# Expert blocks ahead of the routing: rounded products whose remainder is made by an accumulating transfer

## The reference, cut to what matters

```python
q = (hf @ wq).reshape(T, PEER_HEADS, 2, PEER_DQ // 2)
s = jnp.einsum('thcd,hckd->thck', q, subkeys)
v_top, i_top = lax.top_k(s, PEER_TOPK)
cand_s = v_top[:, :, 0, :, None] + v_top[:, :, 1, None, :]
best_s, best_pos = lax.top_k(cand_s, PEER_TOPK)
g = jax.nn.softmax(best_s, axis=-1)
ub = jnp.take(u_tab, ids, axis=0)
act = jax.nn.gelu(jnp.einsum('tkd,td->tk', ub, x))
y = jnp.einsum('tk,tkd->td', g * act, jnp.take(v_tab, ids, axis=0))
```

## Time and profile before

| | |
|---|---|
| median of three runs | 2167.39 us |
| the profiled execution | 2171.05 us |
| its span, first to last instruction | 2169.3 us |
| TensorE busy | 2108.0 us, 97% of the span |
| VectorE busy | 1376.8 us, 63% |
| ScalarE busy | 704.3 us, 32% |
| GpSimd busy | 4.8 us |
| mean granted TensorE clock | 0.986 of full speed |

### The profile page before, as it was taken

The page is one execution under the profiler, slowest core; times in us unless marked ns, Lnnn a source line. Parts: engine busy times, 40 slices in busy tenths (PEclk is TensorE's granted clock), DMA queues, the critical chain, the costliest instruction groups (busy, mean ns, idle before and its releaser), DMA issues.

```text
span 2169.3 us, 31600 instructions
## 1 busy us (share of the span) xinstructions
PE 2108.0 (97%) x12416; PEld 1897.5 (87%) x12416; DVE 1376.8 (63%) x1874; ACT 704.3 (32%) x745; POOL 4.8 (0%) x11
## 2 busy tenths in 40 slices
PE   7999998998999998999999999999999999999997
PEld 5888887887988998999999999989999999999785
DVE  6675575568788986556565655655555565654675
ACT  2014112005311344434334343433434334342432
POOL 0000000000000000000000000000000000000000
PEclk8999999999999999999999999999999999999999
DMA  9999595994443458555555555655555565555552
GB/s 390 421 419 362 197 365 236 380 421 172 171 155 116 180 216 319 206 179 209 188 218 193 195 207 176 219 189 207 204 183 207 186 222 189 200 206 177 196 193 78
DMA packets 98649, 496.12 MB, mean 229 GB/s; under 512 B 8256, under 2 KB 41312, under 8 KB 43040
## 3 DMA queue, kind: packets, MB, share of 16 engines
q1 hardware_dynamic: 83280, 373.81, 45.9%
q10 hardware_dynamic: 14112, 115.35, 14.0%
q0 software_dynamic: 1200, 6.16, 0.7%
HBM read 473.14 MB, written 22.15 MB: 228 GB/s over the span
## 4 chain that ended last, share of the span: by engine, by line
PE 89%; DMA 7%; DVE 3%; ACT 1%; issue 0%; ACTq 0%; DVEq 0%; SPq 0%; POOL 0%
PE ps L470 19%; PE ps L459 11%; PE ps L460 11%; PE ps L461 11%; PE ps L725 5%; PE ps L727 5%; PE ps L726 5%; PE ps L714 5%; PE ps L715 5%; PE ps L716 5%; DMA mod_first<-wmod 4%; PE ps L671 3%; DMA mod_ring<-wmod 1%; DVE mod_first L1112 1%; DMA wraw<-wst 1%; DVE rstd L1088 0%
## 5 line engine op out<-in xcount | busy, mean ns | idle before, releaser
L461 PE MATMUL ps<-h_hi,wlo 128*128 128x256 f32 x1952 | 553.3, 283 | 0.0
L459 PE MATMUL ps<-h_hi,whi 128*128 128x256 f32 x1728 | 490.0, 284 | 5.4 <-ACT act_u L954 5.4
L460 PE MATMUL ps<-h_lo,whi 128*128 128x256 f32 x1728 | 490.0, 284 | 0.0
L1411 DVE TENSOR_TENSOR yacc<-yacc,ps 128x512 f32<-128x512 f32 x256 | 176.1, 688 | 404.5 <-PE ps L727 404.5
L461 PEld LDWEIGHTS ps<-h_hi,wlo 128*128 128x128 f32 x1952 | 375.5, 192 | 0.0
L1377 DVE TENSOR_TENSOR vlo<-vraw,vhi 128x2048 fp32r<-128x2048 f32 x116 | 260.8, 2289 | 135.3 <-ACT vhi L1001 135.3
L459 PEld LDWEIGHTS ps<-h_hi,whi 128*128 128x128 f32 x1728 | 332.7, 193 | 7.6 <-issue 5.6
L460 PEld LDWEIGHTS ps<-h_lo,whi 128*128 128x128 f32 x1728 | 332.7, 193 | 2.0
L470 PE MATMUL ps<-hid,wraw 128*128 128x256 f32 x1344 | 296.6, 381 | 4.7 <-DVE hid L1258 4.7
L470 PEld LDWEIGHTS ps<-hid,wraw 128*128 128x128 f32 x1344 | 256.6, 191 | 40.7 <-issue 4.9
L1373 DVE TENSOR_TENSOR wlo<-wraw,whi 128x2048 fp32r<-128x2048 f32 x120 | 269.4, 2285 | 16.6 <-ACT whi L977 16.6
(11 more groups left out here) (239 smaller groups left out, 2336.1 us busy)
## 6 DMA issues: line engine op xcount, KB each, us to landing
vraw<-vtab SPq DMA_DIRECT2D x116, 1024.0 KB, 6.7
wraw<-wst SPq DMA_DIRECT2D x108, 1024.0 KB, 4.8
wraw<-wst ACTq DMA_DIRECT2D x94, 1024.0 KB, 7.1
mod_ring<-wmod SPq DMA_DIRECT2D x74, 1024.0 KB, 12.6
mod_first<-wmod SPq DMA_DIRECT2D x22, 1024.0 KB, 20.0
gates_dram<-gstage ACTq DMA_DIRECT2D x4, 4096.0 KB, 16.8
gring<-gates_dram SPq DMA_DIRECT2D x64, 256.0 KB, 5.1
wraw<-vtab SPq DMA_DIRECT2D x12, 1024.0 KB, 5.0
```

The source lines that it names most:

```text
L459: mm(dst, hi, src_hi, start=first, stop=False)
L460: mm(dst, hi, src_lo, start=False, stop=False)
L461: return mm(dst, lo, src_hi, start=False, stop=last)
```

## The change

Four constants and orders change. PLAIN = 2 is new, FIRST goes from 12 to 16, EARLY from 20 to 24 (LAG stays 24). Blocks 0 and 1 stay plain. Blocks 2 to 15 are in the rounded form, with the token halves that are there already and with weight halves made in a new way. ScalarE's `early_hi` copies the raw block twice: rounded into `chi`, and negated and rounded into `neg`. GpSimd then issues a DMA that adds the raw block to `neg`, element by element, so that `neg` holds the remainder. There are two buffers of each. The gates are spread in blocks 16 to 23, still plain, and blocks 20 to 23 are no longer in the rounded form. Memory is rearranged for `neg` (`left` shrinks to four half heads, `eqs` moves), and VectorE clears `yacc` only when all spreads are done. In short form, with line numbers left out:

```diff
+PLAIN = 2
-FIRST = 12
-EARLY = 20
+FIRST = 16
+EARLY = 24
...
+            def early_block(b):
+                n = N_U + b
+                pe.wait_ge(s_wev, n - 1)
+                pe.wait_ge(s_elo[b % 2], (b - PLAIN) // 2 * 16 + 16)
+                for kk in range(KD):
+                    r = three(ps_w[n % 2], chi[:, b % 2, kk, :], neg[b % 2][:, kk, :], h_hi[:, kk, :],
+                              h_lo[:, kk, :], kk == 0, kk == KD - 1)
+                r.then_inc(s_wmm, 1)
...
-            for n in range(N_U + 1, N_U + 4):
-                h2_chunk(n % 4, n, 0, n)
-            stretch(pe, N_U + 4, N_U + FIRST, h2_chunk)
+            h2_chunk((N_U + 1) % 4, N_U + 1, 0, N_U + 1)
+            for b in range(PLAIN, FIRST):
+                early_block(b)
...
             def early_gelu(b):
                 n = N_U + b
-                multiplied(n % 4, n, 0, n)
+                if b + W_RING < LAG:
+                    multiplied(n % 4, n, 0, n)
                 gelu(n, n, b)
 
+            def early_hi(b):
+                n = N_U + b
+                act.wait_ge(s_w[n % W_RING], turns(0, n, W_RING) * 16)
+                act.wait_ge(s_wmm, n - 1)
+                A(chi[:, b % 2], wraw[:, n % W_RING], ACT.Copy)
+                A(neg[b % 2][:], wraw[:, n % W_RING], ACT.Copy, scale=-1.0).then_inc(s_neg, 1)
+
             act.wait_ge(s_spill, 16)
+            early_hi(PLAIN)
             early_gelu(0)
             score_out(HC - 1)
+            early_hi(PLAIN + 1)
             for b in range(1, FIRST):
                 early_gelu(b)
+                if PLAIN + 1 < b + 1 < FIRST:
+                    early_hi(b + 1)
...
+            dve.wait_ge(s_gmm, SPREADS)
             own.did(V.memset(yacc[:], 0.0)); own.settle()
...
+            for b in range(PLAIN, FIRST):
+                pool.wait_ge(s_neg, b - PLAIN + 1)
+                pool.dma_start(neg[b % 2][:], wraw[:, (N_U + b) % W_RING],
+                               accum_op=ALU.add).then_inc(s_elo[b % 2], 16)
```

More of the change, by code:

```diff
@@ L188, in hybrid_block @@
         qry = at("qry", 213.5, [4, T])
-        eqs = at("eqs", 205.5, [PEER_H, T])
+        eqs = at("eqs", 77.5, [PEER_H, T])
         k = 77.5
         score = at("score", k, [TT, HC, P]); k += 16
-        left = at("left", k, [TT, HC, P]); k += 16
+        left = at("left", k, [TT, 4, P]); k += 4
+        neg1 = at("neg1", k, [KD, P], F32R); k += 12
         cand = at("cand", k, [PEER_H, T]); k += 8
@@ L203, in hybrid_block @@
         assert k <= 157.5
+        neg = [at("neg0", 149.5, [KD, P], F32R), neg1]
         gstage = at("gstage", 85.5, [2, NB, TW])
@@ L318, in hybrid_block @@
         s_chi, s_clo = sem("chunk_hi_halves"), sem("chunk_lo_halves")
+        s_neg = sem("negated_hi_halves")
+        s_elo = [sem(f"early_lo_added{i}") for i in range(2)]
         s_whi, s_wlo, s_vhi, s_vlo = sem("w_hi_ready"), sem("w_lo_ready"), sem("v_hi_ready"), sem("v_lo_ready")
@@ L1314, in _ @@
                 dve.wait_ge(s_scr, hc + 1)
-                top16([(top_v[:, tt, hc], top_i[:, tt, hc], score[:, tt, hc], left[:, tt, hc]) for tt in range(TT)])
+                top16([(top_v[:, tt, hc], top_i[:, tt, hc], score[:, tt, hc], left[:, tt, hc % 4]) for tt in range(TT)])
             own.settle()
```

## The result

The changed kernel takes 2348.28 us (median of four runs, 2345.45 to 2351.01) against 2166.40 for the kernel before: a ratio of 1.0836, 95% interval 1.0822 to 1.0849. It is slower by 182 us; the forecast was 2368 in a range of 2310 to 2490.

A forecast was written before the change was run, and what follows sets the result against it. TensorE's throughput was taken to bound the kernel. v_group 0 counts from 1014.8 + 35.5 = 1050.3 instead of 849.35, 201 us later; on the profiled 2171.05 that gives 2372, less 3.7 to the median: 2368 us, range 2310 to 2490.

The forecast's parts named there:

- The ring: Blocks 4 to 15: product, gelu, two copies, transfer, product in series without overlap; 21.4 us a turn against 6.91; 12 turns.
- D: Landing time of GpSimd's accumulating DMA into `neg`, 1 MB: 8.5 us, from 1.0 fixed plus 7.5 for reading two operands.
- The product after the wait: TensorE's product in each turn, at a lowered clock after over 13 us idle: 8.0 plus 0.1 for its first matmul.
- The clock's share: Slow clock in the products of the 12 turns: 12 x 2.3 = 28 us.
- The end of block 15: Last early block: 635.7 after block 3, 12 turns of 21.4, one gelu table load of 1.28: ends at 893.8.
- The routing: VectorE's first exponential comes some 80 us late, within over 150 us of slack; TensorE's wait of 3.1 us stays.
- Behind the spreads: From block 23 to v_group 0: 33 us plus 2.5 of slow clock, 35.5 against 42.5; clearing's 4.3 us idle hidden.
- The prediction's 27.3: Microseconds after block 23 at which the second v block lands, on the path from the last gates' store to v_group 0.
- The sum: v_group 0 counts from 1050.3 instead of 849.35, 201 us later, giving 2368 us for the whole kernel.
- From there on both kernels are the same: After the start of v_group 0 the changed kernel takes the same time as the kernel before.
- The slow and the cheap addition: Two rivals on the transfer's landing: 19.6 us, 2512 in all, chance 0.13; 4.8 us without slow clock, 2292, chance 0.04.
- The making runs ahead: Rival: ScalarE and GpSimd keep ahead of TensorE, early blocks go at 5.77 us; 2171, no change; chance 0.03.

The follow-up runs named there:

- three-buffer run: The changed kernel with three buffers for both halves and the copies of block b + 3 behind the gelu of block b: 2198.40 us, ratio 1.0138.

## Why the prediction was right

*The ring.* Right, in its place and in its cause: blocks 2 and 3 made ahead, 12 turns behind them, TensorE waiting for the DMA into `neg`. One edit to the order took 111 us away. Forecast 21.4 a turn and once 1.28 for the gelu table, measured 20.4 with it.

*D.* The term that was mis-sized: 8.5 forecast, 6.9 measured (7.9 and 8.7 for blocks 2 and 3, beside the loads), as doubling the whole growing part on the line through GpSimd's two plain rows was too much. A copy alone lands in 4.2, so the second operand costs 2.7 and not 3.7. The estimate of 6.8 us from the Trainium skill, "DMA: Bandwidth & Descriptors", section "Anatomy of one DMA — SWDGE (gpsimd) path", with "Collectives: The Full Stack", passage "Why ReduceScatter is half of AllGather", agrees with 6.9, and beats mine.

*The product after the wait.* 8.1 forecast, 8.0 measured for block 4; later ones took up to 8.6 (block 6, from 674.6 to 694.7, has TensorE busy for 8.5), which is why the mean turn is 20.4 and not 20.0. So the miss of 1.6 in D was in part made up by some 0.5 here, and the forecast turn was 1.0 too long. The clock's share, 2.3 x 12 = 28, was measured as 29.

*The end of block 15.* Forecast 893.8, measured 878.8; the profiled execution of the changed kernel is 1.4 us ahead already at a load issue before block 0 (600.79, where the earlier trace rows has 602.19), so the error of the step is 13.6.

*The routing.* Right. VectorE waited 197.7 us for the two exponentials, up to 126.5 at once, and TensorE waited for VectorE's picks for the same 3.1 us as before.

```profile
DVE small L1375 <- ACT pick_t L995: 197.7, 2, 126.5
```

*Behind the spreads.* Right in shape, 6.4 us too dear. The clearing put 4.69 us ahead of block 24 (4.3 forecast) and was hidden by the longer wait for the gates (8.51, where some 15 were forecast). v_group 0 started 26.6 after the last spread and not 33: with no block of `u_tab` being loaded beside it, the last store of gates landed in 11.8 us, where I took 16.8. The second block of `v` landed in 7.9 and not 8.6. (The prediction's 27.3 is 27.8 when its four terms are added up, which changes nothing here.) SyncE's next issue shows it, 11.9 after the store at 998.5:

```profile
1010.40 0.38 SPq L397 DMA_DIRECT2D gring<-gates_dram  x1
```

*The sum.* 13.6 from the ring, 6.4 from the gates and 2.2 from the eight blocks with spreads (118.8 us and not 121.0) make the 22 by which the forecast of v_group 0 (1014.8 + 33 = 1047.8, less 1.4) missed 1024.18. All three went the same way, so the forecast is not near the measured time by errors that cancel. "From there on both kernels are the same" holds within a few microseconds: from the first product of v_group 0 to the last product of v it is 1274.5 us, where it was 1271.1, and 2.5 of these 3.4 were forecast as slow clock.

*The rivals.* The slow and the cheap addition fell with D. "The making runs ahead" was held to be excluded by ScalarE's order; the three-buffer run shows that with that order put right a second limit lies behind it, which I had not priced: the DMA engines' own time, 8.1 us a block.

## What to carry to other kernels

A double buffer is worth nothing if the instruction that fills it stands, in its engine's program, behind one that waits for the consumer: read the order of waits on the engine and not the wait at the instruction. Before a remainder or a sum is given to the DMA engines, count their time for it and for the loads in the same stretch against the compute it feeds. Here an addition costs 5.2 us of all 16 engines and wins 1.14 us of TensorE. By the sums it fits at most once in two blocks (5.2 and two loads of 2.9 are 11.0 of 12.7 us); once in three blocks it ran without a wait. And what is won ahead of a stage is kept only as far as the data of its second and third step come sooner too: here three rounded blocks won 3.5 us ahead of the spreads, and the median kept 1.3.

## What had not been expected

- An accumulating transfer of 1 MB within SBUF holds the 16 DMA engines for 5.2 us, against 2.9 for a load of the same size (both estimates from the queues' shares of one window); alone it lands in 6.9, with two buffers filled ahead in 9.0, with three in 12.0.
- GpSimd's subtraction of 128x2048 takes 4.5 us alone and up to 6.8 beside VectorE, and a VectorE multiplication of 2.3 us takes up to 6.6 beside it: the one that begins second waits for the first. A cast of 128x128, 0.23 us otherwise, took 4.68 that way.
- A 4 MB store that lands in 19.1 us beside loads of the table lands in 11.8 without them (13.1 in the run with the moved spreads alone).
